# The opening of a two-block transformer kernel: condition and normed input made in pairs of tiles, one multiplication on GpSimd, four output tiles swept together

## What is computed

```
ada = silu(c) @ w_ada + b_ada                        # c: 1 x 1024, w_ada: 1024 x 6144
shift1, scale1, gate1, shift2, scale2, gate2 = split(ada, 6)
h = rms_norm(x, norm1_g) * (1 + scale1) + shift1     # rms_norm: x * rsqrt(mean(x*x) + 1e-6) * g
proj = h @ w_in                                      # index keys and weights, index queries, k, q, v, conv
ki = rope(rms_norm(ki)); qi = rope(qi); ...          # then index scores, top-128 keys per query, attention
```

## Time and profile before

| | us |
|---|---|
| three runs | 2326.77, 2325.19, 2327.32 (median 2326.77) |
| profiled execution | 2330.56 |
| its span, first to last instruction | 2327.2 |
| TensorE busy | 2236.0 (96%), mean granted clock 0.988 |
| VectorE, ScalarE, GpSimd busy | 1537.8, 1196.3, 290.3 |

### The profile page before, as it was taken

One profiled execution on the slowest core, in us unless ns is written; L12 is line 12 of the kernel. 1 busy time (PEld: TensorE's weight loads), 2 busy tenths in 40 slices (PEclk: granted clock), 3 DMA queues, 4 the chain that ended last, 5 costly groups with the idle time before them and its releaser, 6 DMA issues.

```text
span 2327.2 us, 30551 instructions
## 1 busy us (share of the span) xinstructions
PE 2236.0 (96%) x10242; PEld 1744.9 (75%) x10242; DVE 1537.8 (66%) x2360; ACT 1196.3 (51%) x1774; POOL 290.3 (12%) x248
## 2 busy tenths in 40 slices
PE   7998999899999999997999999999999999999997
PEld 5776676778888888875766788888777776888885
DVE  7788866899999999986654643333446666333334
ACT  4333434688888888884434333323235654223332
POOL 0000000343444333432000000000020000000000
PEclk9999999999999999998999999999999999999999
DMA  8511246799999999995210132233321122322332
GB/s 331 195 55 64 92 165 231 255 364 390 394 393 389 390 391 390 389 356 161 96 49 20 62 114 94 99 99 100 99 91 55 55 63 65 108 92 97 100 108 82
DMA packets 107473, 415.72 MB, mean 179 GB/s; under 512 B 20161, under 2 KB 32705, under 8 KB 82640
## 3 DMA queue, kind: packets, MB, share of 16 engines
q1 hardware_dynamic: 87408, 378.47, 43.4%
q0 software_dynamic: 19504, 34.73, 6.0%
q10 hardware_dynamic: 432, 0.87, 0.1%
HBM read 408.67 MB, written 43.65 MB: 194 GB/s over the span
## 4 chain that ended last, share of the span: by engine, by line
PE 78%; DVE 11%; issue 4%; ACT 4%; DVEq 2%; DMA 1%; SPq 0%; ACTq 0%; POOLq 0%
PE PS L298 22%; PE PS L300 22%; PE PS L299 22%; DVE wl L197 3%; PE PS L724 3%; PE PS L2050 2%; ACT wh L192 2%; PE PS L746 2%; DVE XTl L2103 1%; PE PS L735 1%; DMA ada_wa<-wada 1%; DVEq L1736 1%; PE PS L2075 1%; DVE S2a L778 0%; PE PS L1214 0%
## 5 line engine op out<-in xcount | busy, mean ns | idle before, releaser
L197 DVE TENSOR_TENSOR wl<-raw,wh 128x1024 fp32r<-128x1024 f32 x239 | 292.8, 1227 | 359.3 <-ACT wh L192 353.2
L298 PE MATMUL PS<-HTh,wh 128*128 128x512 f32 x1184 | 473.8, 400 | 7.2 <-ACT V L895 2.2
L197 DVE TENSOR_TENSOR wl<-eraw,wh 128x1024 fp32r<-128x1024 f32 x384 | 457.7, 1219 | 17.1 <-ACT wh L192 13.6
L300 PE MATMUL PS<-HTh,wl 128*128 128x512 f32 x1184 | 462.6, 391 | 0.0
L299 PE MATMUL PS<-HTl,wh 128*128 128x512 f32 x1184 | 462.4, 391 | 0.0
L192 ACT ACTIVATE wh<-eraw 128x1024 fp32r<-128x1024 f32 x384 | 392.6, 1054 | 18.6 <-PE PS L300 16.5
L192 ACT ACTIVATE wh<-raw 128x1024 fp32r<-128x1024 f32 x239 | 251.6, 1055 | 289.9 <-PE PS L300 266.6
L298 PEld LDWEIGHTS PS<-HTh,wh 128*128 128x128 f32 x1184 | 222.9, 188 | 69.4 <-issue 13.0
L300 PEld LDWEIGHTS PS<-HTh,wl 128*128 128x128 f32 x1184 | 222.9, 188 | 47.8
L299 PEld LDWEIGHTS PS<-HTl,wh 128*128 128x128 f32 x1184 | 223.2, 189 | 44.8 <-issue 1.4
L298 PE MATMUL PS<-wh,XTh 128*128 128x512 f32 x536 | 221.1, 413 | 1.9 <-DVE wl L2239 1.4
(11 more groups left out here) (419 smaller groups left out, 3531.8 us busy)
## 6 DMA issues: line engine op xcount, KB each, us to landing
eraw<-wstream SPq DMA_DIRECT2D x192, 1024.0 KB, 9.4
raw<-wstream SPq DMA_DIRECT2D x240, 512.0 KB, 3.3
ada_w<-wada SPq DMA_DIRECT2D x20, 512.0 KB, 5.8
eraw<-wexp SPq DMA_DIRECT2D x9, 1024.0 KB, 8.0
ada_wb<-wada SPq DMA_DIRECT2D x2, 2048.0 KB, 15.6
ada_l<-wada SPq DMA_DIRECT2D x8, 512.0 KB, 3.4
ada_g<-wada SPq DMA_DIRECT2D x2, 2048.0 KB, 10.6
expert_sum<-LM SPq DMA_DIRECT2D x8, 512.0 KB, 5.4
```

Source lines behind the costliest of these rows:

```text
L197: nc.vector.tensor_tensor(wl[:, ci % RING, :], src, wh[:, ci % RING, :].bitcast(F32), ALU.subtract).then_inc(split_done, 1)
L298: nc.tensor.matmul(o, lh, rh, start=start, stop=False)
L300: return nc.tensor.matmul(o, ll, rh, start=False, stop=stop)
```

## The change

- Transfers: the four raw chunks and shift columns 4 and 5 are moved ahead of `ada_wa`.
- The condition is made for two tiles at a time (`condition(pair)`), each behind its own sums, between weight splits and low parts. The shift matmuls of tiles 0, 1 and 2, 3 go to banks 4 and 3, with a signal each. The five matmuls with ones are gone.
- `X * rstd` for the eight tiles is a tensor_tensor on GpSimd, as soon as `rstd` is there. The affine step (times `amul`, plus `cond`) is an activation on ScalarE in place, and a second one rounds it to the high part; VectorE's low part is a plain subtraction.
- The sine of the rope angles moves on ScalarE behind the fourth tile.
- Four weight chunks are split in the opening (`already=1`), and in1 begins with `four_products` over four tiles; the third and fourth use banks 5 and 6 (`spare_bank=5`).

```diff
@@ -165,7 +165,7 @@
         raw_arrived = [sem(f"raw_arrived{i}") for i in range(RING)]
         split_high, split_done, chunk_used = sem("split_high"), sem("split_done"), sem("chunk_used")
         bank_free = [sem("bank_free0"), sem("bank_free1")]
-        bank_free += bank_free
+        bank_free += bank_free + [None] + bank_free
@@ -230,13 +230,13 @@
                 sp.dma_start(ada_wb[:, 4:8, :], wada[4:8].rearrange("c p n -> p c n")).then_inc(scale_in[0], 16)
                 sp.dma_start(ada_wb[:, 0:4, :], wada[0:4].rearrange("c p n -> p c n")).then_inc(shift_in, 16)
                 sp.dma_start(ada_wb[:, 8:10, :], wada[8:10].rearrange("c p n -> p c n")).then_inc(scale_in[1], 16)
+                for c in range(RING):
+                    sp.dma_start(raw[:, c, :], wstream[c]).then_inc(raw_arrived[c], 16)
+                for c in range(2):
+                    sp.dma_start(ada_w[:, c, :], wada[12 + c]).then_inc(ada_in[c], 16)
                 sp.dma_start(ada_wa[:], wada[10:12].rearrange("c p n -> p c n")).then_inc(sem("scale_late"), 16)
-                for c in range(4):
+                for c in range(2, 4):
                     sp.dma_start(ada_w[:, c, :], wada[12 + c]).then_inc(ada_in[c], 16)
-                for c in range(2):
-                    sp.dma_start(raw[:, c, :], wstream[c]).then_inc(raw_arrived[c], 16)
-                for c in range(2, RING):
-                    sp.dma_start(raw[:, c, :], wstream[c]).then_inc(raw_arrived[c], 16)
             sp.dma_start(K[:, CONST_EARLY:CONST_N], consts[:, CONST_EARLY:CONST_N]).then_inc(sem("consts_late"), 16)
...
 
-        def four_products(pe, c0, u0, rhs, k_ready, order, spare_free=None):
+        def four_products(pe, c0, u0, rhs, k_ready, order, spare_free=None, spare_bank=2):
 
             for t, c in order:
-                b = (u0 + c) % 2 + c // 2 * 2
+                b = (u0 + c) % 2 + c // 2 * spare_bank
                 if c == 0:
...
@@ -1049,13 +1049,13 @@
                                      stop=m == DT - 1).then_inc(n_used, 1)
                 pe.wait_ge(sem("csil"), 1)
                 pe.wait_ge(shift_in, 16)
-                for m in range(4):
-                    for kt in range(DT):
-                        mm = nc.tensor.matmul(PS[:, 4, m:m + 1], ada_k[kt][:, m * P:(m + 1) * P], csil[:, kt:kt + 1],
-                                              start=kt == 0, stop=kt == DT - 1)
-                mm.then_inc(sem("shifts"), 1)
-                for _ in range(5):
-                    nc.tensor.matmul(PS[:, 6, :], const("ones"), sq[:, 1, :], start=True, stop=True)
+                for pair in range(2):
+                    for m in range(2):
+                        a = 2 * pair + m
+                        for kt in range(DT):
+                            mm = nc.tensor.matmul(PS[:, 4 - pair, m:m + 1], ada_k[kt][:, a * P:(a + 1) * P],
+                                                  csil[:, kt:kt + 1], start=kt == 0, stop=kt == DT - 1)
+                    mm.then_inc(sem("shifts"), 1)
 
             @stage("act")
             def _(act):
@@ -1070,63 +1070,88 @@
                 nc.scalar.activation(rstd[:], PS[:, 7, :], ACT.Ln, bias=const("eps6"), scale=1.0 / D)
                 act.drain()
                 nc.scalar.activation(rstd[:], rstd[:], ACT.Exp, scale=-0.5).then_inc(n_root, 1)
-                act.wait_ge(sem("ang"), 1)
-                nc.scalar.activation(CS[:, 0, :], CS[:, 0, :], ACT.Sin)
-                nc.scalar.activation(CS[:, 1, :], CS[:, 1, :], ACT.Sin)
-                act.drain().then_inc(sem("sin"), 1)
-                for c in range(2):
-                    split_act(act, c)
+                def columns_in(m):
+                    act.wait_ge(n_mul, ml0 + m + 1)
+                    act.wait_ge(sem("condition"), m // 2 + 1)
+                    nc.scalar.activation(HF[:, m, :], HF[:, m, :], ACT.Identity, bias=cond[:, m:m + 1], scale=amul[:, m:m + 1])
+                    act.drain()
+                    nc.scalar.activation(Hh(m), HF[:, m, :], ACT.Copy).then_inc(n_high, 1)
+
+                split_act(act, 0)
+                split_act(act, 1)
                 for m in range(DT):
-                    act.wait_ge(n_mul, ml0 + m + 1)
-                    nc.scalar.activation(Hh(m), HF[:, m, :], ACT.Identity, bias=cond[:, m:m + 1],
-                                         scale=1.0).then_inc(n_high, 1)
-                    if m == 0:
-                        split_act(act, 2)
+                    columns_in(m)
+                    if m in (1, 2):
+                        split_act(act, m + 1)
+                    if m == 3:
+                        act.wait_ge(sem("ang"), 1)
+                        nc.scalar.activation(CS[:, 0, :], CS[:, 0, :], ACT.Sin)
+                        nc.scalar.activation(CS[:, 1, :], CS[:, 1, :], ACT.Sin)
+                        act.drain().then_inc(sem("sin"), 1)
+
+            @stage("pool")
+            def _(pool):
+                pool.wait_ge(n_root, rt0 + 1)
+                for m in range(DT):
+                    nc.gpsimd.tensor_tensor(HF[:, m, :], Xm(m), rstd[:], ALU.mult).then_inc(n_mul, 1)
 
             @stage("dve")
             def _(dve):
+                b_at, g_at = COL_AT["b_ada"][0], COL_AT["norm1_g"][0]
+
+                def scale_sums(*tiles):
+                    for a in tiles:
+                        ada(dve, ada_t[a], 8 + a)
+
+                def shift_sums(*tiles):
+                    for a in tiles:
+                        dve.wait_ge(ada_in[a - 4], 16)
+                        ada(dve, ada_w[:, a - 4, :], a)
+
+                def condition(pair):
+                    a = 2 * pair
+                    dve.drain()
+                    nc.vector.tensor_tensor(cond[:, 8 + a:10 + a], adac[:, 8 + a:10 + a], C[:, b_at + 8 + a:b_at + 10 + a], ALU.add)
+                    if pair < 2:
+                        dve.wait_ge(sem("shifts"), pair + 1)
+                    nc.vector.tensor_tensor(cond[:, a:a + 2], PS[:, 4 - pair, 0:2] if pair < 2 else adac[:, a:a + 2],
+                                            C[:, b_at + a:b_at + a + 2], ALU.add)
+                    dve.drain()
+                    nc.vector.scalar_tensor_tensor(out=amul[:, a:a + 2], in0=cond[:, 8 + a:10 + a], scalar=1.0,
+                                                   in1=C[:, g_at + a:g_at + a + 2], op0=ALU.add,
+                                                   op1=ALU.mult).then_inc(sem("condition"), 1)
+
+                def rest(m):
+                    dve.wait_ge(n_high, hg0 + m + 1)
+                    nc.vector.tensor_tensor(Hl(m), HF[:, m, :], Hh(m).bitcast(F32), ALU.subtract).then_inc(norm_out, 1)
+
                 rope_angles(dve)
                 dve.wait_ge(sem("csil"), 2)
                 dve.wait_ge(scale_in[0], 16)
-                for a in range(4):
-                    ada(dve, ada_t[a], 8 + a)
+                scale_sums(0, 1, 2, 3)
                 dve.wait_ge(scale_in[1], 16)
-                for a in range(4, 6):
-                    ada(dve, ada_t[a], 8 + a)
+                scale_sums(4, 5)
+                split_dve(dve, 0)
+                condition(0)
+                split_dve(dve, 1)
+                rest(0)
+                rest(1)
+                split_dve(dve, 2)
+                condition(1)
+                rest(2)
+                split_dve(dve, 3)
+                rest(3)
+                shift_sums(4, 5)
+                condition(2)
                 dve.wait_ge(sem("scale_late"), 16)
-                for a in range(6, 8):
-                    ada(dve, ada_t[a], 8 + a)
-                for a in range(4, 8):
-                    dve.wait_ge(ada_in[a - 4], 16)
-                    ada(dve, ada_w[:, a - 4, :], a)
-                dve.wait_ge(ada_used, 12)
-                a = COL_AT["b_ada"][0]
-                nc.vector.tensor_tensor(cond[:, 8:16], adac[:, 8:16], C[:, a + 8:a + 16], ALU.add)
-                dve.drain()
-                g = COL_AT["norm1_g"][0]
-                nc.vector.scalar_tensor_tensor(out=amul[:, 0:8], in0=cond[:, 8:16], scalar=1.0, in1=C[:, g:g + 8],
-                                               op0=ALU.add, op1=ALU.mult)
-                dve.wait_ge(sem("shifts"), 1)
-                nc.vector.tensor_tensor(cond[:, 0:4], PS[:, 4, 0:4], C[:, a:a + 4], ALU.add)
-                nc.vector.tensor_tensor(cond[:, 4:8], adac[:, 4:8], C[:, a + 4:a + 8], ALU.add)
-                dve.drain()
-
-                dve.wait_ge(n_root, rt0 + 1)
-
-                def scaled(m):
-                    nc.vector.scalar_tensor_tensor(out=HF[:, m, :], in0=Xm(m), scalar=amul[:, m:m + 1], in1=rstd[:],
-                                                   op0=ALU.mult, op1=ALU.mult).then_inc(n_mul, 1)
-                scaled(0)
-                split_dve(dve, 0)
-                for m in range(DT):
-                    if m + 1 < DT:
-                        scaled(m + 1)
-                    dve.wait_ge(n_high, hg0 + m + 1)
```

(22 more changed lines are left out.)

## The result

The changed kernel takes 2337.48 us (median of 6 runs, 2335.34 to 2340.01) against 2326.49 (2324.55 to 2327.37) for the kernel before on the same chip: ratio 1.0048, 95% interval 1.0035 to 1.0061. It is slower by 11.0 us where 5.8 were forecast, and half a microsecond above the range. The profiled execution took 2335.70 us, 1.8 round its span.

A forecast was written before the change was run, and what follows sets the result against it. VectorE's making of the inputs bounds the opening, after which TensorE sets the pace. Term one (−1.5) and term two (+7.3) sum to +5.8 on the 2326.77 median: 2332.6 us, range 2325.0 to 2337.0.

The forecast's parts named there:

- Term two: Opening: the eight GpSimd multiplications stop VectorE's two-input work for 10.4 us, of which 7.3 land on the path: +7.3.
- exclusion: Opening: VectorE's two-SBUF-input instructions stand still until GpSimd's whole instruction is over; main case, +5.8 in all, chance 0.60.
- The opening without contention: Opening, if GpSimd cost VectorE nothing: last low part ends at 51.35, half 5 (chunk 5's low half) at 56.4.
- 18.3 us of VectorE's work … with nothing to wait for: 74.7: From chunk 5's low half at 56.4 to the first rope's end: VectorE works 18.3 us without waits, ending at 74.7.
- Behind it … TensorE's chain is unchanged: Behind the second rotation: TensorE's chain stays unchanged to the end and a shift there passes through.
- Rival three: Opening: idle TensorE falls to half clock on top of contention; if that lasts to 52, +9, 2335.8; chance 0.07.
- Term one: Edits without contention: TensorE stands 6 us ahead at chunk 4, then stalls 4.2 for the first rope: −1.5.
- Rival one: Opening: no exclusion, GpSimd yields and all stands as in term one, 2325.3; chance 0.20.
- Rival two: Opening: partial exclusion, VectorE keeps the port and GpSimd takes its waits; delay 3 to 4, +2, 2328.8; chance 0.10.
- Rival four: After the opening: the whole 6 us lead survives, VectorE's work between 56 and 75 us being off the path, 2320.9; chance 0.03.
- the rope's wait: Ahead of the second rotation: TensorE waits some 4 us for the first rope.

The follow-up runs named there:

- experiment 1: Changed kernel without the eight GpSimd multiplications (ScalarE reads X itself): 2337.9 us, ratio 1.0051; total of no use, four extra expert blocks instead of three.
- experiment 5: Kernel before plus eight two-input multiplications on GpSimd beside VectorE's opening, result not used: 2334.63 us, ratio 1.0036.
- experiment 2: Changed kernel with the twelve late condition columns transferred by half: 2573.56 us, ratio 1.1053; total unreadable, 18 extra expert blocks.
- Experiment 4: Changed kernel with the sixteen late condition columns spread over steps 2 to 10 of in1 instead of 2 to 9: 2329.2 us, ratio 1.0013.
- experiment 9: Experiment 7's kernel with the sixteen late condition columns two a step in steps 3 to 10: 2321.16 us, ratio 0.9977 against the kernel before.
- experiment 7: Changed kernel with the multiplications on VectorE instead of GpSimd and one ScalarE activation a tile: 2330.55 us, ratio 1.0022 against the kernel before.
- experiment 3: Changed kernel with seven products with ones on TensorE ahead of its second rotation: 2333.63 us, ratio 1.0032 against the kernel before.
- experiment 12: Experiment 9's kernel without the sweep of four tiles (in1 begins with two tiles together): 2329.92 us, ratio 1.0015 against the kernel before.
- experiment 8: Experiment 7's kernel with the late condition columns also spread over steps 2 to 10: 2326.11 us, ratio 0.9997 against the kernel before.

## Why the forecast had the direction and not the size

- **Term two, exclusion: right.** Two-input work of both engines takes turns (experiments 1 and 5). Priced at 7.3; measured 6.0 at the last low part, and 7.8 at the rope with a wait for columns that differs from run to run (experiment 1). The form differs a little: each turn costs VectorE about 1.05 us, not 1.3, and GpSimd's eight need 14.8 us, not 10.4. Nor does every instruction of VectorE wait: the low half at 32.90 took 1.21 with GpSimd at work. TensorE's first large matmul came at 35.84 (forecast 36 to 37).
- **The opening without contention: 1.1 us too short.** The last low part ends at 52.50 (forecast 51.35), half 5 starts at 57.98 (56.4). With the smaller 6.0 above this cancelled, so that 58.7 and 63.7 were met to 0.3 is in part luck.
- **The first step that failed: "18.3 us of VectorE's work … with nothing to wait for: 74.7".** It took 18.3 plus the waits for columns: 19.7 without GpSimd, 21.45 with it, and 18.0 with half the bytes (experiment 2), where no wait was left. I took VectorE's waits for ScalarE out of its work without asking whether the queues could feed it. Four instructions of it (three sums and the low half of a chunk, 65.17 to 70.12) use four transfers of 512 KB in 4.95 us, 424 GB/s; the queues had shown 408 and gave 374 on average in 72 to 80 us. The last two columns ahead of the rope landed 7.8 and 7.9 us after their issue. The queues also start late: a column is fetched only when a sum has freed its place, the first at 66.42, and from 64 to 68 us they moved 20 and 74 GB/s. In the kernel before, I take the 2.7 us in which VectorE waited for ScalarE for the queues' slack; no run shows that alone. Experiment 4, and 9 against 7, fit: with fewer columns in steps 2 to 4 the wait goes.
- **The second: "Behind it … TensorE's chain is unchanged", wrong by 1.65.** The wait that I forecast myself brought the lower clock behind it (experiment 3). Rival three looked for the low clock in the opening. There it lasted to about 44.5 (0.50 in 43 to 44 us, 0.72 in 44 to 45), inside the stretch that the rival calls hidden; no run prices it.
- **Sum.** Term one is +3.5 instead of −1.5 (experiment 1): 1.6 for the later half 5, 1.5 for the wait for columns, 1.7 for the clock and 0.2 of small change. Term two is +7.8 instead of +7.3, so the two together are +11.3 at the third rotation and the scatter (+11.0 in the medians) instead of +5.8. Rivals one, two and four are refuted by the rows of VectorE and the wait of 7.18. The direction was right because exclusion and the rope's wait were; that the size missed the range by only 0.5 owes something to the errors that cancelled.
- **The sweep** does what term one says: it puts TensorE ahead, and VectorE's sums in steps 2 to 4 take that lead back. Without it the pairs are 8.8 us slower (experiment 12); with it, with the sums placed later and with nothing on GpSimd, 5.3 us are left against the kernel before.

## What to carry to other kernels

When a wait of a dense engine is removed, price the supply too: bytes used per microsecond of its new pace against what the queues have shown. A stall forecast for TensorE needs a second term for the clock behind it. Before two-input elementwise work goes to GpSimd, count VectorE's two-input SBUF instructions beside it; each may wait for a whole instruction (here 1.06 us a time).

## What the runs showed of the hardware that I had not expected

- Turns go by instruction, not by size: an addition of 128x2 or 128x8 waits 0.9 us as a sum of 128x1024 waits 1.06, while one that reads PSUM took its 0.15 with GpSimd at work (one row, at 31.68 us).
- One SBUF input on GpSimd costs VectorE 0.40 us on every second sum, and GpSimd up to 1.0 on its own instruction (1.51 to 2.51).
- A wait of TensorE of 1.39 us left the granted clock at 1.00; waits of 2.08, 3.72, 5.41, 6.47 and 7.18 (experiments 8, 2, 1, 7 and the changed kernel) went with 0.50 and with 1.6 to 2.1 us more from one rotation to the next. Seven products of 512 columns in the wait removed that cost.
- The same list of VectorE's work waited 1.49, 1.82, 2.52 and 3.14 us for columns in four profiled runs (experiments 1, 3, 7 and the changed kernel).
